# First mixer: attention steps take in the grouped heads' projection, the transpositions and most of the output projection

## The reference, cut to what matters

```python
xn = _rms_norm(x, attn_norm[l])
h = xn @ w_in[l]          # cq 384, ckv 256, kr 32, dq 512, dk 512, dv 512, gq 384, gk 128, gv 128
# latent heads (6): q from norm(cq) @ w_uq, k (64 of 96) and v from norm(ckv) @ w_ukv, k's other 32 from kr
# differential heads (4): two maps each, softmax(q0 k0) - lam * softmax(q1 k1), v 128 wide, normed
# grouped heads (6 on 2 keys): axial rotation
# all: q and k get an RMS norm a head, a gain and a rotation; softmax over the 256 keys
mix = concatenate([o_a, o_b, o_c])         # 384 + 512 + 384 = 1280
x = x + mix @ w_o[l]
xn = _rms_norm(x, ffn_norm[l])
x = x + (silu(gate) * up) @ w_down[l]
```

## Time and profile before

| | |
|---|---|
| median of three runs | 2569.75 us |
| profiled execution, its own time | 2568.69 us |
| its span from first to last instruction | 2566.9 us |
| TensorE matmuls, busy | 2358.2 us (92%) |
| VectorE busy | 1809.4 us (70%) |
| ScalarE busy | 1436.2 us (56%) |
| mean granted clock of TensorE | 0.94 |
| layer 0's first mixer, first product to last of the output projection | 25.4 to 248.9 us |
| layer 1's | 453.1 to 675.5 us |
| its first attention scores, layer 0 and layer 1 | 118.15 and 545.78 us |

### The profile page before, as it was taken

How to read it: one execution, slowest core, us unless ns; L and a number is a source line. 1 busy time by engine, 2 the same in 40 slices (tenths; PEclk the granted TensorE clock), 3 DMA queues, 4 the chain that set the end, 5 groups by cost and what they waited for, 6 DMA issues and landing times. The chain is left out here.

```text
span 2566.9 us, 30070 instructions
## 1 busy us (share of the span) xinstructions
PE 2358.2 (92%) x11132; PEld 1970.0 (77%) x11132; DVE 1809.4 (70%) x2497; ACT 1436.2 (56%) x2065; POOL 76.7 (3%) x71
## 2 busy tenths in 40 slices
PE   6788999967899899899989879999999999999997
PEld 5677787757788778678877777888888888888885
DVE  4955555784555556655555647989898989898987
ACT  4433444442444444444444436878787878787875
POOL 0200000110000100000010000000000000000000
PEclk9867999985899999999999969999999999999998
DMA  6402555420455553445553326999999999999996
GB/s 238 135 1 83 195 188 182 148 90 1 150 188 188 186 169 103 140 166 191 185 186 122 123 82 240 368 340 369 340 377 338 371 347 368 341 371 341 365 347 234
DMA packets 157176, 570.81 MB, mean 222 GB/s; under 512 B 18497, under 2 KB 18817, under 8 KB 156385
## 3 DMA queue, kind: packets, MB, share of 16 engines
q1 hardware_dynamic: 153424, 553.48, 61.1%
q0 software_dynamic: 3600, 15.35, 1.8%
HBM read 567.71 MB, written 1.05 MB: 222 GB/s over the span
## 5 line engine op out<-in xcount | busy, mean ns | idle before, releaser
L369 DVE TENSOR_TENSOR w_lo<-raw,w_hi 128x1024 fp32r<-128x1024 f32 x1051 | 1270.0, 1224 | 444.0 <-ACT w_hi L363 416.6
L363 ACT CAST w_hi<-raw 128x1024 fp32r<-128x1024 f32 x1051 | 1098.9, 1052 | 474.4 <-PE bank L417 453.7
L415 PE MATMUL bank<-w_hi,x_hi 128*128 128x512 f32 (+1 forms) x2864 | 1136.4, 397 | 44.0 <-DVE x_lo L455 23.7
L417 PE MATMUL bank<-w_hi,x_lo 128*128 128x512 f32 (+1 forms) x2864 | 1116.1, 390 | 0.0
L416 PE MATMUL bank<-w_lo,x_hi 128*128 128x512 f32 (+1 forms) x2864 | 1114.2, 389 | 0.0
L415 PEld LDWEIGHTS bank<-w_hi,x_hi 128*128 128x128 f32 x2864 | 544.8, 190 | 154.1 <-issue 25.0
L417 PEld LDWEIGHTS bank<-w_hi,x_lo 128*128 128x128 f32 x2864 | 543.3, 190 | 113.0
L416 PEld LDWEIGHTS bank<-w_lo,x_hi 128*128 128x128 f32 x2864 | 545.6, 191 | 104.1
L748 PE MATMUL bank<-arena,PT 128*128 128x64 f32 (+1 forms) x576 | 96.2, 326 | 2.2 <-DVE O L765 2.2
L706 ACT ACTIVATE PP<-bank,small 128x256 f32<-128x256 f32 x80 | 37.2, 470 | 107.8 <-DVE small L696 107.8
L748 PEld LDWEIGHTS bank<-arena,PT 128*128 128x128 f32 x576 | 93.6, 247 | 2.6 <-DVE PT L735 2.4
(11 more groups left out here) (185 smaller groups left out, 1391.6 us busy)
## 6 DMA issues: line engine op xcount, KB each, us to landing
raw<-in_stream SPq DMA_DIRECT2D x1051, 512.0 KB, 5.7
tab<-in_lngb POOLq DMA_DIRECT2D x5, 1024.0 KB, 5.2
arena<-in_rpb POOLq DMA_DIRECT2D x16, 256.0 KB, 5.1
arena<-in_bgate POOLq DMA_DIRECT2D x4, 512.0 KB, 4.6
tab<-in_rowv POOLq DMA_DIRECT2D x2, 640.0 KB, 9.2
X<-in_x SPq DMA_DIRECT2D x1, 1024.0 KB, 5.4
out_y<-X SPq DMA_DIRECT2D x2, 512.0 KB, 2.9
tab<-in_ropec POOLq DMA_DIRECT2D x2, 448.0 KB, 5.1
```

What stands on the lines that cost most here:

```text
L363: nc.scalar.copy(w_hi[:, s % SPLIT, :], raw[:, slot, :]).then_inc(hi_done, 1)
L369: e.tensor_tensor(w_lo[:, s % SPLIT, :], raw[:, s % RAW, :], w_hi[:, s % SPLIT, :].bitcast(F32), ALU.subtract).then_inc(lo_done, 1)
L415: pe.matmul(out, xh, wh, start=first, stop=False)
L417: return pe.matmul(out, xl, wh, start=False, stop=last)
```

## The change

The order of the columns of H is regrouped into seven chunks: cq (384), ckv with kr (288), dq, dk, dv (512 each), gq (384), gk with gv (256). That is 26 halves a layer instead of 24. The last two chunks are no longer computed ahead of the attention but inside it, in steps 0 to 6 and 8 to 10. The latent blocks are transposed beside dq's chunk, the up-projections stand between dk's and dv's chunk (the stream is reordered to match), and dk is rotated beside the first of them. The latent maps now come ahead of the grouped maps. In the attention all PT copies are ScalarE's, O has one bank, the transposed probabilities one, and ahead of every unit and filler TensorE waits for the copy of map k-1. Steps 6 to 11 have the latent units, 12 and 13 those of the grouped heads, 13, 15, 17, 18 and 20 those of O; steps 14 to 21 have eight halves of the output projection, and two follow. The gain of the differential heads is moved out of VectorE's row operation into the scale of the transposed blocks (`og_col`). The FFN's transpositions use two banks. The second mixer takes the new units and bank 3 for O.

```diff
...
 def chunks_in1():
-    return [(c, min(512, W_IN1 - c)) for c in range(0, W_IN1, 512)]
+    return [(C_CQ, MQR), (C_CKV, MKVR + MROPE), (C_DQ, 2 * DH * DQ), (C_DK, 2 * DH * DQ), (C_DV, DH * DV),
+            (C_GQ, GH * GD), (C_GK, 2 * GKV * GD)]
...
+        order[b:b + H_O] = [b + k for k in O_ORDER]
     for x in range(1, NE):
         a = MOE_AT + x * H_EXP
...
+        def unit(E, bk, dst, srcs, w=P, scale=1.0, gains=None, lag=1):
+            e = E.e
+            hi, lo = dst
+            nb = len(srcs)
+            pb = bank[bk][0:w, 0:nb * S]
+            p3 = pb.rearrange("p (b n) -> p b n", n=S)
+            if E.kind == "pe":
+                wait(e, qk_lo, E.qk.at(1 - lag))
+                for b, src in enumerate(srcs):
+                    for tb in range(TB):
+                        i = e.transpose(pb[:, b * S + tb * P:b * S + (tb + 1) * P], src(tb), ident[:, :])
+                i.then_inc(qk_full, 1)
+            if E.kind == "act":
+                e.wait_ge(qk_full, E.qk.at(1))
+                if gains is None:
+                    i = nc.scalar.mul(hi, p3, scale)
+                else:
+                    for b in range(nb):
+                        i = nc.scalar.activation(hi[:, b, :], p3[:, b, :], ACT.Copy, scale=gains[:, b:b + 1])
+                i.then_inc(qk_hi, 1)
+            if E.kind == "dve":
+                e.wait_ge(qk_hi, E.qk.at(1))
+                if gains is None:
+                    i = e.scalar_tensor_tensor(lo, p3, scale, hi.bitcast(F32), ALU.mult, ALU.subtract)
+                else:
+                    for b in range(nb):
+                        i = e.scalar_tensor_tensor(lo[:, b, :], p3[:, b, :], gains[:, b:b + 1],
+                                                   hi[:, b, :].bitcast(F32), ALU.mult, ALU.subtract)
+                i.then_inc(qk_lo, 1)
+            E.qk.n += 1
...
@@ -709,22 +725,20 @@
                 m = step - 1
                 if 0 <= m < M:
                     g = E.map.at(m)
-                    tbk = bank[2 if packed else 2 + m % 2]
+                    tbk = bank[2]
                     if E.kind == "pe":
                         e.wait_ge(p_ready, g + 1)
-                        if packed:
-                            if m:
-                                e.wait_ge(*copied(m - 1))
-                        else:
-                            wait(e, (pt_act, pt_dve)[m % 2], g // 2)
+                        if m:
+                            e.wait_ge(*copied(m - 1))
+                        e.wait_ge(qk_lo, E.qk.at())
                         for kb in range(TB):
...
                                 i = e.transpose(tbk[:, kb * S + tb * P:kb * S + (tb + 1) * P],
                                                 PP[:, m % 2, tb, kb * P:(kb + 1) * P], ident[:, :])
                         i.then_inc(pt_full, 1)
-                    if E.kind == ("act", "dve")[m % 2]:
...
                         e.wait_ge(*copied(m))
-                        wait(e, o_done, g + 1 - (1 if packed else 3))
+                        wait(e, o_done, g)
...
-                if aside:
-                    aside(step)
+                if units:
+                    if E.kind == "pe" and 0 < step < M + 1:
+                        e.wait_ge(*copied(step - 1))
+                    units(step)
+                aside(step)
...
+            def latent_rows(kn, n, b0, tiles, dst, j, aside):
+                if E.kind == "act":
+                    need_rs(E)
+                if E.kind == "pe":
+                    e.wait_ge(qk_lo, E.qk.at())
+                    wait(e, acc_act, E.acc.at())
+                    wait(e, acc_dve, E.acc.at())
...
+            def beside_dq(hx):
+                if hx == 0:
+                    latent_squares()
+                if hx == 1:
+                    latent_blocks()
+                if hx == 2:
+                    gain_column()
+            def beside_dk(hx):
+                if hx < 3:
+                    rotate(hx, C_DQ, F_DQ, at_q)
+            def beside_uq(hx):
+                rotate(hx, C_DK, F_DK, at_k)
+            def beside_dv(hx):
+                if hx == 2:
+                    if E.kind == "pe":
+                        e.wait_ge(acc_act, E.acc.at())
+                        e.wait_ge(acc_dve, E.acc.at())
+                    diff_blocks(C_DK, DH)
+            chunk(0, nothing)
+            chunk(1, nothing)
+            chunk(2, beside_dq)
+            chunk(3, beside_dk)
+            diff_blocks(C_DQ, 0)
+            latent_rows(nq, MH * MQK // 2, 4, pair_of(b_cq, nq), QA, at_l, beside_uq)
             if E.kind == "pe":
...
-            blocks = [(j, blk(H, C_DQ + j * P, P), P) for j in range(2 * DH)]
-            nb = 2 * DH
-            gg = GH // GKV
...
+            def out_half(n):
+                def use(wh, wl):
...
+                    return i
+                if E.kind == "pe":
+                    e.wait_ge(qk_lo, E.qk.at())
+                    if n == 0:
+                        e.wait_ge(acc_act, E.acc.at())
+                        e.wait_ge(acc_dve, E.acc.at())
+                E.half_step(use)
+            def out_unit(bk, k, n, map_end, scale=1.0, lag=1):
+                if E.kind == "pe":
+                    e.wait_ge(o_done, E.map.at(map_end))
+                unit(E, bk, (x_hi[:, k:k + n, :], x_lo[:, k:k + n, :]), [blk(O, (k + i) * P) for i in range(n)],
+                     scale=scale, lag=lag)
+            def units(step):
+                if 6 <= step < 6 + MH:
+                    h = step - 6
+                    if E.kind == "pe":
+                        e.wait_ge(qk_src, E.qks.at())
+                        if step == 8:
+                            e.wait_ge(acc_act, E.acc.at())
+                            e.wait_ge(acc_dve, E.acc.at())
+                    bk = 2 if step < 8 else 4 + step % 2
+                    unit(E, bk, pair_of(place(2 * h), 2, MQK), [blk(QA, h * MQK, MQK), blk(KA, h * MQK, MQK)], w=MQK)
+                if step == 12 or step == 13:
+                    j = 2 * (step - 12)
+                    if E.kind == "pe":
+                        e.wait_ge(qk_src, E.qks.at())
+                    unit(E, 4 + step % 2, pair_of(b_gq + j), [blk(H, C_GQ + (j + i) * P) for i in range(2)])
+                if step == 13:
+                    if E.kind == "act":
+                        e.wait_ge(og_done, l + 1)
+                    if E.kind == "dve":
+                        e.wait_ge(og_done, l + 1)
+                    for j in range(2):
+                        out_unit(4 + j, 3 + 2 * j, 2, 2 * DH, scale=og_col[:, 0:1])
+                if step == 15:
+                    out_unit(2, 0, 2, 2 * DH + 4)
+                if step == 17:
+                    out_unit(2, 2, 1, 2 * DH + 6)
+                if step == 18:
+                    out_unit(2, 7, 1, 2 * DH + 8)
+                if step == 20:
+                    out_unit(2, 8, 1, 2 * DH + 10)
+            gq, gkv = column_halves(5, 4), column_halves(6, 6)
+            def fill(step):
+                if step in (0, 2, 4, 6, 7):
+                    next(gq, None)
+                if step in (8, 10, 11):
+                    next(gkv, None)
+                if step >= 14:
+                    out_half(step - 14)
+                if step < 6:
+                    latent_heads(step)
+                if step in (7, 8, 9):
+                    grouped(step - 7, C_GQ, GH, F_GQ, at_g)
+                if step == 10:
+                    diff_norm(0)
+                if step == 11:
+                    diff_norm(1)
+                    grouped(0, C_GK, GKV, F_GK, at_g + TB * GH)
+                if step == 12:
+                    grouped(1, C_GK, GKV, F_GK, at_g + TB * GH)
+                    grouped(2, C_GK, GKV, F_GK, at_g + TB * GH)
             maps = []
             for h in range(DH):
...
+            attention(E, maps, fill, act_copies=True, units=units)
+            out_unit(2, 9, 1, 0)
+            for n in (8, 9):
+                out_half(n)
             if E.kind == "dve":
                 e.wait_ge(w_used, E.st.done(-1))
-            add_to_x(E, 1.0, bank[0:4])
-            norm_transposes(E, colg[:, l, CG_FFN:CG_FFN + KD], 4)
+            add_to_x(E, 1.0, bank[4:8])
+            norm_transposes(E, colg[:, l, CG_FFN:CG_FFN + KD], (2, 3))
...
```

More of the change, by code:

```diff
@@ L118, in stream_order @@
     order = list(range(TOTAL))
+    late = sum(halves_of(w) for _, w in chunks_in1()[4:])
+    for l in range(LAYERS):
+        a = l * H_L1 + H_IN1 - late
+        b = l * H_L1 + H_IN1 + H_UQ + H_UKV
+        n = H_UQ + H_UKV
+        order[a:b] = list(range(b - n, b)) + list(range(a, b - n))
+        order[b:b + H_O] = [b + k for k in O_ORDER]
     for x in range(1, NE):
@@ L417, in mm3, with tp_stage @@
             return pe.matmul(out, xl, wh, start=False, stop=last)
[L420 removed]
+        def tp_stage(E, src, blocks, k0, gain=None, parts=1, banks=(4, 5, 6, 7)):
             e = E.e
@@ L643, in attention, with by_act @@
+            E.qk.n += 1
```

(10 more changed lines are left out.)

343 lines of the change are left out of this document (185 added, 158 removed).

## The result

The kernel after takes 2609.61 us (median of four runs, 2608.19 to 2611.31), the kernel before 2568.75 in four runs on the same chip. The ratio is 1.0156, with a 95% interval of 1.0139 to 1.0174: slower, by 41 us or 1.6%. The forecast was 2606 in a range of 2565 to 2640. The profiled execution took 2609.08, its span is 2607.2 us against 2566.9, and the mean granted clock 0.944 against 0.940.

The account below looks back on a forecast made before the run. The first mixer's attention was taken as a chain of waits on in-order TensorE, with a slow clock. Per layer -16 + 24 (attention and output projection) + 9 + 1.3 = +18.3, twice +36.6, gave 2606 us; range 2565 to 2640.

Parts of the forecast that it names:

- the sum: Layer total of the terms for the attention's start, its stage, the clock and the FFN's banks: +18.3 us, twice +36.6.
- Ahead of the attention, -16: Projections before layer 0's first scores: scores start at 101 to 102 instead of 118.15, 16 us earlier a layer.
- Steps 0 to 5: First mixer's attention: VectorE's rotations stand behind low splits, 9.7 us more, so the scan of step 6 comes at 33.
- Steps 6 to 13: First mixer's attention, unit steps at full clock: 61 us in sum, scores of step 14 at 94 us.
- strict chain: Attention steps counted with scan, copy, unit, splits and VectorE passes one after another; better overlap was the lower bound, +12.
- Steps 14 to the end: Attention's last steps and output projection: plain step 6.4 us, unit steps up to 8.6, together 61, end at 155.
- The clock, +9, bounds 0 and 20: First mixer's attention stage: TensorE's lower clock adds 9 us a layer, at most 16 in steps 0 to 13.
- FFN's banks, +1.3: Transpositions ahead of the FFN with two banks for four: the third pair waits for the first's low part, +1.3 us.
- The second mixer, 0: Second mixer: units do two blocks in one instruction, under 0.3 us, and banks are renamed; no change.
- The rival of the filled pipeline: First mixer's attention: copies and units finish before TensorE needs them, plain steps 5.14 us, stage 134, total 2547; 16%.
- The rival with the clock up throughout: First mixer's stage: the clock stays up, first scores to end of projection in 155 us, total 2588; 17%.
- the slow one: First mixer's stage: the lower clock holds for most of it, +20 us instead of 9, total 2628; 12%.

Follow-up runs that it names:

- the early high split: Kernel after the change, but in steps with a weight half ScalarE makes the high part before the step's exponentials and copy: 2601.16 us, 1.013 to the kernel before.
- The dummies: Kernel after the change plus five unused 512-column matmuls in each of steps 1 to 12 of the first mixer's attention: 2608.39 us, 1.0147 to the kernel before.
- the four edits: Kernel after, copy wait only for bank 2 units, half not behind the new low part, high split first, kv products not behind q evacuation: 2545.12 us, 0.9896.

## Why the prediction was right, point by point

Layer 0's first FFN product moved from 252.76 to 270.96: +18.2 us, the sum had +18.3. Layer 1 moved by 20.4, not by the same again, mostly because its stage before the change was 1 us shorter than layer 0's and its start gained 1 us less. The two make 38.5 of the 40.3 by which the spans differ. That the sum comes so close to layer 0 is in part luck, as the terms show:

- **Ahead of the attention, -16.** The scores start at 103.37, so -14.8. The mechanism was right: TensorE stands idle for 5.87 us behind the q columns' evacuation. The experiment that lifts that wait brings the first scores 7 us forward, which also shows that it was a new cost of the change and not inevitable.
- **Steps 0 to 5.** The scan of step 6 was to come 33 us after the first scores; 136.31 - 103.37 = 32.9. Behind low splits, as said; the early high split moves them.
- **Steps 6 to 13.** Scores of step 14 were put at 94 us, all at full clock; they start 198.89 - 103.37 = 95.5 after the first, with the clock at 0.76. Step 13 was sized 9.2 and took 198.89 - 186.44 = 12.4: its units follow one another at 2.9 and 2.7 us instead of 2.2. The other steps were 1.5 to 2 us cheaper together than the strict chain.
- **Steps 14 to the end.** Plain step 6.4: measured 6.46. Step 17: 7.8 for 8.2. Step 14 was to be 6.4 and took 208.38 - 198.89 = 9.5, step 15 8.6 and took 10.9, step 18 8.2 and took 9.4, all three partly at the lower clock (0.56, 0.69 and 0.82 from scan to scan). From the scores of step 14 to the end it is 66.6 us for 61.
- **The clock, +9, bounds 0 and 20.** The stage, first scores to end of the projection, took 265.47 - 103.37 = 162.1 us. The sum had 155 + 9 = 164. If the 155 is taken as it stands, the clock's part is 7. The size came out, the place did not. The prediction allowed at most 16 us for steps 0 to 13 and some 4 later. Measured against its full-clock chain, steps 0 to 13 are 1.5 us longer and the rest 5.6. The dummies bear this out: of steps 3 to 8, put at 1.00, only step 4 of layer 1 is shorter by more than 0.3 us. Behind step 14 the same step with a unit takes 7.8, 9.4 or 10.4 us with the clock. Nor is clock a price of the waits alone. In the second mixer a wait of 1.24 us is shown to cost 2.94. In the first, the kernel without the copy's wait in steps 8 to 14 has the same clock in steps 9 to 13, and the kernel before, with TensorE busy for 26.84 of 27.00 us, has 0.50. What brings the clock down in the first mixer stays open.
- **FFN's banks, +1.3.** 270.96 - 266.85 = 4.1 instead of 2.5: +1.6.
- **The second mixer, 0.** In layer 0 the additions around it are 215.4 us apart instead of 213.2, in layer 1 215.2 instead of 215.3, in one profile each. What the 2.2 us are was not tested.

The rival of the filled pipeline (2547) was wrong for this kernel and nearly right for its neighbour, the one with the four edits at 2545: its plain steps take 5.1 us and its units mostly hide behind halves (6.6 to 6.8 us a step, once 8.2). But that rival put all on the wait for the copy, and lifting this wait alone gave 2587; it took the low part's wait, the kv wait and the early high split as well. And from first scores to the addition to X it is 140 and 137 us there where the rival had 134, with an attention that starts 4 to 5 us earlier than it had, so that the total agrees partly by chance. The rival with the clock up throughout (2588) wanted a stage of 155 us and got 162.1; the slow one (2628) failed because the clock came back with the halves (1.00 in steps 16 and 17, 0.95 from 240 us).

## What to carry to other kernels

Work that is moved into a waiting loop pays for every wait that stands ahead of it: place a wait at the instruction that needs it, not ahead of a whole group, and keep one unit in flight by a second bank. Look at where in its own engine's queue the awaited instruction stands; the same copy made TensorE wait 1.1 to 2.1 us behind ScalarE's exponentials and 0.2 to 0.5 behind VectorE's scan. When such an edit fails to pay, count its waits in one step before giving up the idea: here one and the same regrouping is 1.6% slower as first written, 1.0% faster with three waits eased and the high split early, and 1.7% faster with the banks and every second copy on VectorE besides. And compare step by step, with the clock of each step beside it: here step 17 changed by 2.6 us with the clock alone, and most of steps 3 to 8 by no more than 0.3.

## What was unexpected of the hardware

A pause of 1.24 us on TensorE was followed by products at the lower level of its clock (0.63 us instead of 0.39 for 512 columns) in a stretch that before had been at 1.00 throughout. The pause's length alone does not decide it: behind 1.69 us the products went at 0.39 to 0.40 twice in the same layer, and so they did behind 1.08 us in step 16 of the kernel after. The Trainium skill (TensorE: Matmul & The Clock Gate, section A second HAM failure mode: psum-queue depth-cycling) tells of short pauses between groups of matmuls that are frequent enough to bring the clock down again and again; the 0.63 us rows of the second mixer agree with that. And more matmuls are no cure by themselves: five dummies a step raised the clock from 0.59 to 0.74 in steps 9 to 13 and left the time where it was.
